# Weight sums of the feed-forwards' first groups on GpSimd, and another order at the experts' beginning

## The reference

```python
def conv_glu_ffn(xn, w_up, conv_w, conv_b, w_down):
    u, gt = split_cols(xn @ w_up, (D_FF, D_FF))        # D_FF = 2752
    u = causal_dwconv(u, conv_w, conv_b)               # three taps
    return (jax.nn.silu(u) * gt) @ w_down

def expert_block(args):                                # in moe_ffn, 32 experts
    xblk, e = args
    hg = xblk @ w_gu[e] + b_gu[e]
    x_glu, x_lin = hg[:, :D_FF_2], hg[:, D_FF_2:]      # D_FF_2 = 1024
    x_glu = jnp.minimum(x_glu, SWIGLU_LIMIT)
    x_lin = jnp.clip(x_lin, -SWIGLU_LIMIT, SWIGLU_LIMIT)
    act = x_glu * jax.nn.sigmoid(SWIGLU_ALPHA * x_glu) * (x_lin + 1.0)
    return act @ w_down[e] + b_down[e]
```

## Time and profile before

| | us |
|---|---|
| median of 3 runs (lowest to highest) | 2172.19 (2171.77 to 2172.55) |
| the profiled execution, its own time | 2178.56 |
| its span | 2176.7 |
| TensorE busy | 2035.7 (94%) |
| VectorE busy | 724.7 (33%) |
| ScalarE busy | 408.3 (19%) |
| GpSimd busy | 111.7 (5%) |
| mean granted clock of TensorE, share of full | 0.974 |

### The profile page before, as it was taken

One profiled execution on the slowest core, in us unless ns is written; L12 is line 12 of the kernel. 1 busy time (PEld: TensorE's weight loads), 2 busy tenths in 40 slices (PEclk: granted clock), 3 DMA queues, 4 the chain that ended last, 5 costly groups with the idle time before them and its releaser, 6 DMA issues.

```text
span 2176.7 us, 29861 instructions
## 1 busy us (share of the span) xinstructions
PE 2035.7 (94%) x12586; PEld 1380.6 (63%) x12586; DVE 724.7 (33%) x1372; ACT 408.3 (19%) x788; POOL 111.7 (5%) x186
## 2 busy tenths in 40 slices
PE   9999999999999999999999999977699999998975
PEld 6888788999888888998777733322243333333422
DVE  5445433775364137774344321100011111000101
ACT  4322132221042122220232410100000010000001
POOL 0123100000000000000000000100000000001000
PEclk9999999999999999999999999988899999999987
DMA  6221343346524436448433499999999999999997
GB/s 266 112 78 41 156 165 116 145 165 232 209 78 155 155 124 233 176 170 347 155 124 141 174 389 427 427 428 426 427 427 414 427 426 427 426 427 427 427 424 308
DMA packets 44589, 587.90 MB, mean 270 GB/s; under 512 B 5392, under 2 KB 5664, under 8 KB 9504
## 3 DMA queue, kind: packets, MB, share of 16 engines
q1 hardware_dynamic: 44448, 585.92, 66.1%
HBM read 584.85 MB, written 1.05 MB: 269 GB/s over the span
## 4 chain that ended last, share of the span: by engine, by line
PE 67%; DMA 28%; DVE 3%; ACT 1%; issue 1%; SPq 0%; DVEq 0%; ACTq 0%
PE pb L412 66%; DMA arena<-in_gu 8%; DMA ring<-in_gu 6%; DMA kv<-in_gu 5%; DMA arena<-in_dne 4%; DMA kv<-in_dne 3%; DMA ring<-in_dne 2%; DVE arena L314 1%; PE pb L422 1%; DVE arena L329 1%; DVE ring L314 0%; ACT arena L373 0%; DMA ring<-in_ab_small 0%; DVE xs L314 0%; DVE arena L323 0%
## 5 line engine op out<-in xcount | busy, mean ns | idle before, releaser
L412 PE MATMUL pb<-arena,ring 128*128 128x256 f32 (+3 forms) x2816 | 527.8, 350 | 7.0 <-DVE xs L314 3.9
L412 PEld LDWEIGHTS pb<-arena,ring 128*128 128x128 f32 (+2 forms) x2816 | 461.2, 191 | 65.8 <-issue 8.9
L412 PE MATMUL pb<-arena 128*128 128x128 f32 (+14 forms) x3804 | 459.3, 324 | 25.6 <-DMA arena<-in_dne 10.8
L412 PEld LDWEIGHTS pb<-arena 128*128 128x128 f32 (+5 forms) x3804 | 342.3, 162 | 126.9 <-issue 97.3
L412 PE MATMUL pb<-arena,cst 128*64 128x512 f32 (+6 forms) x1108 | 274.9, 610 | 42.0 <-DMA ring<-in_gu 26.4
L412 PE MATMUL pb<-ring,cst 128*64 128x512 f32 (+2 forms) x784 | 246.5, 626 | 8.8 <-DMA arena<-in_gu 4.2
L412 PEld LDWEIGHTS pb<-arena,cst 128*64 128x64 f32 (+4 forms) x1108 | 88.7, 140 | 195.1 <-issue 192.8
L412 PE MATMUL pb<-ring,arena 128*64 128x512 f32 (+4 forms) x640 | 171.4, 538 | 22.4 <-DMA arena<-in_dne 17.3
L321 DVE TENSOR_SCALAR arena<-pb 128x512 f32<-128x512 f32 x30 | 20.8, 692 | 460.7 <-PE pb L412 460.7
L379 ACT ACTIVATE arena<-pb 128x512 f32<-128x512 f32 (+2 forms) x146 | 72.8, 499 | 518.6 <-PE pb L422 391.6
L412 PEld LDWEIGHTS pb<-ring,cst 128*64 128x64 f32 (+2 forms) x784 | 73.7, 138 | 130.4 <-issue 130.4
(11 more groups left out here) (162 smaller groups left out, 1612.0 us busy)
## 6 DMA issues: line engine op xcount, KB each, us to landing
arena<-in_gu SPq DMA_DIRECT2D x64, 2048.0 KB, 19.4
ring<-in_gu SPq DMA_DIRECT2D x49, 2048.0 KB, 19.4
arena<-in_dne SPq DMA_DIRECT2D x30, 2048.0 KB, 19.4
ring<-in_dne SPq DMA_DIRECT2D x22, 2048.0 KB, 19.4
kv<-in_gu SPq DMA_DIRECT2D x15, 2048.0 KB, 19.5
ring<-in_up SPq DMA_DIRECT2D x14, 2048.0 KB, 8.1
kv<-in_dne SPq DMA_DIRECT2D x8, 2048.0 KB, 19.5
ring<-in_wkv SPq DMA_DIRECT2D x7, 2048.0 KB, 7.9
```

The lines of the kernel that those rows point to most:

```text
L412: r = self.e.matmul(out, lhsT, rhs, start=start, stop=stop, skip_group_check=True)
```

## The change

Four edits.

1. GpSimd gets a program `ffn_g` for each feed-forward: after the attention's last product (`xa{n}.o3`) it makes all four weight sums of groups 0 and 1. VectorE makes those of groups 2 to 9 only. The order of the two programs is that of the first and second feed-forward, then the experts.
2. ScalarE copies FIRST of group 1 ahead of the taps of group 0.
3. `route_g` makes all GM maps of a job before the GGM maps, with a mark for each; the transposes of GGM (`gates_p`) are a step of their own and stand, in the first job, between the first and second expand. In the first job the biases stand ahead of the gather, each half of the first expand waits for its half of the gathered tokens, and the warm-up ahead of them is two products instead of five.
4. Unit e0.gu00.0 is loaded into the ring and e0.gu10.1 into the place that is filled once; the first half of the first job uses other memory (`DEAD`) as scratch.

```diff
+        def ffn_g(G, n):
+            G.begin(f"ffn{n}")
+            G.wait_ge(f"xa{n}.o3")
+            for g in range(2):
+                weight_sums_v(G, f"up{n}.{g}", SPARE[n][g], (1, 3, 4))
...
             tap(LAST)
             silu(LAST)
+            first(1)
             tap(0)
             for g in range(1, SEVENS):
-                first(g)
+                if g > 1:
+                    first(g)
...
-                if g < SEVENS:
+                if 1 < g < SEVENS:
...
-            sums(0, 1)
             root_v(V, f)
-            sums(0, 3, 4)
             halved_v(V, f, (f"{f}.u{LAST}", f"{f}.g{LAST}"))
...
                     last_in()
-                    sums(1, 1)
...
                     V.mark(f"{m}.c11")
-                    sums(1, 3)
                     gated(before)
...
+            if n != JOBS[0]:
+                gates_p(P, n)
+
+        def gates_p(P, n):
             b = P.tile(f"{n}.s")
+            P.wait_ge(f"{n}.ggm")
...
-                maps_g(lane, slice(g * width, (g + 1) * width), [rank[:, i, e:e + 1] for i in range(2)],
-                       [gate[:, i, e:e + 1] for i in range(2)])
+            for o, ranks, gates in parts:
+                maps_g(lane, o, ranks)
             lane.mark(n + ".gm")
+            for o, ranks, gates in parts:
+                weighted_g(lane, o, ranks, gates)
+            lane.mark(n + ".ggm")
...
+        def up_biases_p(P, n, k, sel):
             b = [P.tile(f"{n}.h{k}{gl}", hold=True) for gl in range(2)]
...
+            if (n, k) == (JOBS[0], 0):
+                P.wait_ge("load bg16", "mo.s0")
+                b = up_biases_p(P, n, k, sel)
+                route_p(P, q, n)
+                ready = [f"free {n}.x{half}" for half in range(2)]
...
+                if ready is not None and c % 4 == 0:
+                    P.wait_ge(ready[c // 4])
...
-            P.warm("mo.w2", ident, cst["tri"], 5)
-            route_p(P, 0, JOBS[0])
+            P.warm("mo.w2", ident, cst["tri"], 2)
...
                     if late is not None:
                         turn_act_p(P, late, 1)
+                    else:
+                        gates_p(P, n)
...
-                    if (u, g) != (0, 0):
+                    if (u, g) != (2, 1):
...
-                F.once(ONCE, f"{JOBS[0]}.gu00.0", (0, 128, dram["gu"][f[0] * 4]), "mo.t11")
+                F.once(ONCE, f"{JOBS[0]}.gu10.1", (0, 128, dram["gu"][f[1] * 4 + 2]), "mo.t11")
```

More of the change, by code:

```diff
@@ L2489, in sums @@
             def sums(g, *which):
-                if g < SEVENS:
-                    weight_sums_v(V, f"up{n}.{g}", SPARE[n][g % 2], which, f"used up{n}.{g - 2}" if g > 1 else None)
+                if 1 < g < SEVENS:
+                    weight_sums_v(V, f"up{n}.{g}", SPARE[n][g % 2], which, f"used up{n}.{g - 2}")
             def last_in():
@@ L3209, in route_g, with maps_g, weighted_g @@
             rank, gate = (RK, GT) if n[0] == "e" else (RKP, GTP)
-            for g, e in enumerate(GROUPS[n]):
-                maps_g(lane, slice(g * width, (g + 1) * width), [rank[:, i, e:e + 1] for i in range(2)],
-                       [gate[:, i, e:e + 1] for i in range(2)])
+            parts = [(slice(g * width, (g + 1) * width), [rank[:, i, e:e + 1] for i in range(2)],
+                      [gate[:, i, e:e + 1] for i in range(2)]) for g, e in enumerate(GROUPS[n])]
+            for o, ranks, gates in parts:
+                maps_g(lane, o, ranks)
             lane.mark(n + ".gm")
-        def maps_g(lane, o, rank, gate):
+            for o, ranks, gates in parts:
+                weighted_g(lane, o, ranks, gates)
+            lane.mark(n + ".ggm")
+        def maps_g(lane, o, rank):
             for i in range(2):
                 lane.ts(GM[:, i, o], cst["iota"][:, 0:o.stop - o.start], rank[i], None, ALU.is_equal, None)
+        def weighted_g(lane, o, rank, gate):
+            for i in range(2):
                 lane.ts(GGM[:, i, o], cst["iota"][:, 0:o.stop - o.start], rank[i], gate[i], ALU.is_equal, MUL)
@@ L3221, in units_of, with expand_p @@
             return [f"{n}.{what}.{g}" for g in range(count)]
-        def expand_p(P, b, x, units, first, sig):
+        def expand_p(P, b, x, units, first, sig, ready=None):
             width = 128 // len(units)
@@ L3279, in narrow_parts_p @@
                 scattered(1, part, f"free {n}.d1{part}")
-        def up_p(P, n, q, k, count, sel, between=None):
+        def up_biases_p(P, n, k, sel):
             b = [P.tile(f"{n}.h{k}{gl}", hold=True) for gl in range(2)]
-            P.wait_ge("load bg16", f"free {n}.s", f"{n}.gm", "mo.s0")
             for gl in range(2):
@@ L3286, in up_p @@
                 P.mm(b[gl], sel[rows, :], BG[rows, :], True, False, sig=f"{n}.b{k}" if gl else None)
+            return b
+        def up_p(P, n, q, k, count, sel, between=None):
+            ready = None
+            if (n, k) == (JOBS[0], 0):
[4 more added lines that the diff above has]
+            else:
+                P.wait_ge("load bg16", f"free {n}.s", f"{n}.gm", "mo.s0")
+                b = up_biases_p(P, n, k, sel)
             for gl in range(2):
@@ L3289, in up_p, with scratch_of @@
                     between()
-                expand_p(P, b[gl], xgs[q], units_of(n, f"gu{k}{gl}", count), False, f"{n}.h{k}{gl}")
+                expand_p(P, b[gl], xgs[q], units_of(n, f"gu{k}{gl}", count), False, f"{n}.h{k}{gl}",
+                         None if gl else ready)
             P.release(f"{n}.h{k}0")
             P.release(f"{n}.h{k}1")
+        def scratch_of(n, k):
+            if (n, k) == (JOBS[0], 0):
+                return [DEAD[:, D + h * 512:D + h * 512 + 512] for h in range(2)]
+            return tmp[k]
         def up_v(V, n, k, before, between=None):
-            t1, t2 = tmp[k]
+            t1, t2 = scratch_of(n, k)
             b = V.tile(f"{n}.h{k}0")
@@ L3316, in up_s @@
             S.wait_ge(f"free {n}.h{k}0")
-            S.act(sg, tmp[k][0], ACT.Sigmoid, scale=1.702)
+            S.act(sg, scratch_of(n, k)[0], ACT.Sigmoid, scale=1.702)
             S.mark(f"{n}.sg{k}")
         def turn_act_p(P, n, k):
-            a = tmp[k][1]
+            a = scratch_of(n, k)[1]
             b = P.tile(f"{n}.t{k}")
@@ L3544, in round_v @@
             picked_v(V, r)
-            maps_g(V, slice(0, 128), [RC[:, i:i + 1] for i in range(2)], [GC[:, i:i + 1] for i in range(2)])
+            ranks, gates = ([t[:, i:i + 1] for i in range(2)] for t in (RC, GC))
+            maps_g(V, slice(0, 128), ranks)
             V.mark(n + ".gm")
+            weighted_g(V, slice(0, 128), ranks, gates)
+            V.mark(n + ".ggm")
             up_v(V, n, 0, None)
@@ L3699, in gpsimd @@
             rwkv_g(G)
+            ffn_g(G, 0)
+            ffn_g(G, 1)
             moe_g(G)
```

## The result

| | before | changed |
|---|---|---|
| median of 10 runs, us | 2172.18 | 2177.74 |
| lowest to highest | 2169.76 to 2174.73 | 2175.68 to 2179.15 |
| the profiled execution, its own time | 2178.56 | 2177.92 |

The changed kernel is **slower by 5.6 us** between the medians. I had predicted 7.5 us faster. Measured again the ratio was 1.0019 (1.0008 to 1.0030).

The account below looks back on a forecast made before the run. TensorE's order of work was taken to bound the kernel up to about 1260 us, the experts' weight loads after. Terms -11.3 + 2.0 + 1.8 = -7.5 us, from 2172.19 to 2164.7 us; range 2160.5 to 2168.8.

Parts of the forecast that it names:

- The gain, -11.3: Both feed-forwards: 3.4 us of TensorE waits saved in each, and half-clock stretches of 2.73 and 1.74 us gone.
- contention, "+2.0 us, bounds 0 and +5.8": Feed-forwards' beginnings: GpSimd slows VectorE's two-SBUF-input operations, 0.8 us for each added_v and 0.4 for halved_v.
- The 0.4 us taken for halved_v: Second feed-forward: halved_v's first operation, on which p1 waits, is slowed beside GpSimd; bound 0.8 us.
- GpSimd in time: Both feed-forwards: GpSimd's eight sums, ending by 368 and 841.8 us, are ready before TensorE wants them.
- the cover of 13 us: Second feed-forward: sums ready at 825.7 and 836.4 us, wanted by the p6 products at 838.8 and 849.5.
- Experts, +1.8: Experts' beginning: later first expand 0.1, transposes 0.45, half clock 1.7, less 0.45 of lead; bounds 0.1 and +4.7 us.
- the gap seven loads on: Experts' weight loads: the early transfer gap moves to seven loads behind the first expand and isn't saved.
- 1.7 taken: Experts' biases and gather: half clock after 3.4 us of idle TensorE costs +1.7 us, bounds 0 and +4.6.
- the lead of 0.45 us: Experts' loads: two slots free when the first expand ends remove the early gap, subtracting 0.45 us.
- C: Rival: contention and clock near upper bounds, 4.5 and 4.0 us, give -2.8, 2169.4 us; 14%.
- D: Rival, slower: GpSimd is late in the second feed-forward and TensorE waits; at 6.5 us per sum, 2180 us; 3%.
- A: Rival: bank free in time, the experts' beginning gains 3.2 us; with clean feed-forwards -13.5, 2158.7 us; 7%.

Follow-up runs that it names:

- base: The kernel before, without any edit, profiled again: ratio 0.9998 (0.9989 to 1.0007), profiled span 2172.9 us.
- after_again: The changed kernel, all four edits, measured again against the kernel before: ratio 1.0019 (1.0008 to 1.0030), +5.4 us between the medians.
- beside: The kernel before with all VectorE's sums, plus useless GpSimd subtractions, four in the first feed-forward and eight in the second: ratio 1.0068, +15.4 us.
- experts_bank: The kernel before with the experts' part alone, VectorE copying the count and freeing mo.rk's bank ahead of the maps: ratio 0.9990 (0.9978 to 1.0002).
- ffn_only: The change without its edits 3 and 4, so the feed-forwards' part alone, against the kernel before: ratio 0.9998 (0.9989 to 1.0008).
- ffn_split: The kernel before with only some sums of groups 0 and 1 on GpSimd, timed to avoid VectorE's two-SBUF-input operations: ratio 0.9960, -6.2 us between medians.
- both: ffn_split and experts_bank together, against the kernel before: 2161.23 us, ratio 0.9942 (0.9924 to 0.9960).

## Why the prediction was wrong

**The gain, -11.3: right.** Group 0 to group 2's p6 takes 27.55 and 27.57 us (868.43 - 840.86), where I forecast 27 to 28.5, down from 34.1 and 33.1: -12.1 against the profile I used. Against `base`, where the half clock was cheaper (33.0 for the first), it is -11.0.

**The failed step: contention, "+2.0 us, bounds 0 and +5.8".** It is 11.7 us in the profile of the changed kernel, and 10.2, worked out the same way, in after_again, where the clock held in the first feed-forward. In `base` the adds take 2.33 us from start to end (361.60 to 363.93), and unit 10's products 7.33:
```profile
361.60 1.49 DVE L314 TENSOR_TENSOR xs<-xs 128x512 f32<-128x512 f32 x2
363.24 0.69 DVE L314 TENSOR_TENSOR xs<-xs 128x512 f32<-128x512 f32 x1 [0.16 <-ACT xs L373]
365.05 7.33 PE L412 MATMUL pb<-arena 128*64 128x256 f32 x48
```
First feed-forward: 4.68 less 2.33, 2.35 us; TensorE's sum and unit 10's products 1.52 + 8.57 instead of 1.09 + 7.33, 1.67 of half clock. Second: 7.77 less 2.33, 5.44; and 2.07 + 8.61 instead of 1.10 + 7.33, 2.25. The 0.4 us taken for halved_v didn't come: GpSimd was done by then.

I made two mistakes in it. I read the row of 2.05 us at 110.54 as a surcharge of 0.83 per operation. GpSimd's row there ends at 103.56 + 7.95 = 111.51: the VectorE operation had begun 0.97 us ahead of that, when most of GpSimd's last operation had already passed. The row showed the tail of a wait and not a price. An operation with both inputs in SBUF waits for the rest of the GpSimd operation under way; beside back-to-back ones of 128x1024 that made 1.6 to 2.0 us for each (2.28 to 2.64 against 0.69, 3.18 and 3.26 against 1.23), and `beside` shows it without the rest of the change. The adds alone, 7.8 us, are past my bound. And I priced the idle time without the clock behind it, 3.9 of the 11.7 us, though the earlier trace rows stood for just that, and I charged it at the experts.

The Trainium skill, "GPSIMD Engine Reference", 8 Key points, says that GpSimd shares its SBUF interfaces with VectorE and contends with VectorE instructions that have two SBUF inputs. The traces here agree in kind: the three adds took 4.68 and 7.77 us instead of 2.33. The prediction had that; the size was what failed.

The same stretch of the profile I used holds a row that would have warned me, of the last of GpSimd's three operations:
```profile
108.07 1.22 DVE L329 SCALAR_TENSOR_TENSOR arena<-arena 128x1024 f32<-128x1024 f32 x1
108.09 3.42 POOL L314 TENSOR_TENSOR arena<-arena 128x1024 f32<-128x1024 f32 x1
```
VectorE began 0.02 us earlier and took its usual time; GpSimd took 3.42 us, 1.07 more than its 2.35. In both directions the one that began later was held up.

**GpSimd in time: right.** Nothing waited for POOL. That it ran early was the harm: the cover of 13 us that I counted was the room in which its work could have been put elsewhere.

**Experts, +1.8: mechanism right, size short.** The wait of 3.31 us for the COPY, the biases in it, the gap seven loads on all came. Measured +2.5 alone, +3.3 to +3.4 in the whole. The clock cost 1.6 alone (1.7 taken) and more in the whole, where also all of the biases and more of the gather ran slow (2.07 and 5.27 us against 1.56 and 5.01). Without the clock the loss was 0.9, against 0.1 + 0.45 - 0.45: the first expand came 0.4 later behind the COPY (5.16 against 4.76) and not 0.1, and the lead of 0.45 us that I subtracted didn't show by 1394 us.

**The sum, redone:** -11 to -12, + 11.7, + 3.3 gives +3 to +4. The medians say +5.6, the ratio +4.8 (2.8 to 7.0); what lies between is open. Of my rivals C had the cause, too small; D, the slower one, had another. A was right that a bank free in time would gain about 3 us, which the change doesn't do; experts_bank does it and gains 2.5 in its stage.

**The profile's 6.4 us above the median:** `base`, itself 1.1 above its median, lies 3.8 us below that profile. Between them are half-clock draws in the mixers (1.6 and 2.8), which don't touch the sum, and one of 1.1 in the first feed-forward, which does: it is in the 2.73 that I priced the half clock with.

## What to carry to other kernels

Before work goes to GpSimd, list what VectorE does in the same stretch. Here its operations with both inputs in SBUF each waited for the rest of the GpSimd operation under way, up to 2.0 us; those with one input in PSUM didn't. Moving eight operations of each feed-forward gained nothing; moving three or four, at the right moments, gained 6 to 9 us in all. When a wait is put at a place where TensorE has no other work, add the clock behind it; and when products are reordered into new PSUM banks, look who frees those banks last.

## What was unexpected of the hardware

- A VectorE add of 128x512 takes 0.69 us alone and 2.28 to 2.64 beside a row of GpSimd operations of 128x1024; GpSimd's own go from 2.35 to 2.67 us, and to 3.22 beside VectorE's of 128x1024. Four operations of 256 columns with one input from PSUM take 1.79 us with and without.
- Two executions of one kernel can agree to 0.01 us over hundreds of microseconds and differ by 1.1 to 1.7 us at a place where the clock falls in one only. Subtracting the starts of the same matmuls told effects of 0.1 us apart, where the ratios of some ten runs are good to about 2 us either way.
- After 2.15 us of idle time TensorE fell to half clock in one profile (8.57 us for unit 10's products) and after 1.93 to 2.06 not in two others (7.33), though in `ffn_only` it did after 2.06 (9.01). Behind the wait of 2.13 us in ffn_split two products ran 1.6 us longer, behind 2.14 in `both` they didn't. What decides it the runs don't show.
